# Inverse root by Ln and Exp on ScalarE, and the shift of the fp32 residual moved out of the tile chain

## The reference

```python
def layer_norm(x, g, b):
    mu = jnp.mean(xf, axis=-1, keepdims=True)
    var = jnp.mean(jnp.square(xf - mu), axis=-1, keepdims=True)
    y = (xf - mu) * lax.rsqrt(var + LN_EPS) * g + b
...
    x = layer_norm(DEEPNORM_ALPHA * x + mix, ln_g[i, 0], ln_b[i, 0])
    if i % 2 == 0:
        ff = swiglu(x, ffn_w_gu[i // 2], ffn_w_down[i // 2])
    else:
        ff = moe_swiglu(x, moe_w_router[i // 2], moe_w_gu[i // 2], moe_w_down[i // 2])
    x = layer_norm(DEEPNORM_ALPHA * x + ff, ln_g[i, 1], ln_b[i, 1])
    x = x + (p[i] @ ple_w_proj[i]) * jax.nn.sigmoid(x @ ple_w_gate[i])
```

## Time and profile before

| | |
|---|---|
| median of 3 runs | 1476.85 us (1471.23 to 1479.42) |
| the profiled execution | 1471.44 us |
| its span, first to last instruction | 1469.7 us |
| TensorE busy | 1324.6 us (90%) |
| VectorE busy | 648.9 us (44%) |
| ScalarE busy | 565.9 us (39%) |
| GpSimd busy | 150.0 us (10%) |

### The profile page before, as it was taken

One profiled execution on the slowest core, in us unless ns is written; L12 is line 12 of the kernel. 1 busy time (PEld: TensorE's weight loads), 2 busy tenths in 40 slices (PEclk: granted clock), 3 DMA queues, 4 the chain that ended last, 5 costly groups with the idle time before them and its releaser, 6 DMA issues.

```text
span 1469.7 us, 17566 instructions
## 1 busy us (share of the span) xinstructions
PE 1324.6 (90%) x6495; PEld 1106.7 (75%) x6496; DVE 648.9 (44%) x906; ACT 565.9 (39%) x783; POOL 150.0 (10%) x106
## 2 busy tenths in 40 slices
PE   7999879799999999998899998797879899988648
PEld 6889778488888878867787896673768798877537
DVE  5333554633333322336433337445553443455565
ACT  3222542632322322236332224234454554466642
POOL 0000000000000000000000000000233532255400
PEclk9999999999999999999999999897789999999869
DMA  6332003133333333203356520020685776588841
GB/s 186 103 101 87 15 15 87 34 97 105 94 99 101 102 99 98 73 29 115 86 92 81 83 76 1 29 65 9 210 263 188 258 230 197 181 275 283 315 158 58
DMA packets 197914, 175.46 MB, mean 119 GB/s; under 512 B 7201, under 2 KB 178273, under 8 KB 197857
## 3 DMA queue, kind: packets, MB, share of 16 engines
q1 hardware_dynamic: 194016, 160.53, 38.0%
q0 software_dynamic: 3312, 12.06, 2.2%
q10 hardware_dynamic: 528, 2.10, 0.4%
HBM read 164.71 MB, written 9.96 MB: 119 GB/s over the span
## 4 chain that ended last, share of the span: by engine, by line
PE 77%; DVE 7%; issue 6%; ACT 4%; DMA 3%; POOL 2%; POOLq 0%; SPq 0%; ACTq 0%; DVEq 0%
PE bank L705 24%; PE bank L706 23%; PE bank L707 23%; POOL w_lo L663 2%; PE bank L798 1%; DMA raw<-ple_w_gate 1%; DMA raw<-moe_w_down 1%; DVE rstd L1682 1%; PE bank L1017 1%; PE bank L872 1%; DVE w_lo L1598 1%; DMA x_tok<-x 1%; PE bank L876 1%; DVE sp L1784 0%; PE bank L934 0%
## 5 line engine op out<-in xcount | busy, mean ns | idle before, releaser
L1598 DVE TENSOR_TENSOR w_lo<-raw,w_hi 128x1024 fp32r<-128x1024 f32 (+5 forms) x215 | 300.5, 1404 | 317.0 <-ACT w_hi L1213 165.4
L705 PE MATMUL bank<-x_hi,w_hi 128*128 128x512 f32 x672 | 265.2, 395 | 15.6 <-DVE x_lo L1598 11.4
L706 PE MATMUL bank<-x_lo,w_hi 128*128 128x512 f32 x672 | 263.9, 393 | 0.0
L707 PE MATMUL bank<-x_hi,w_lo 128*128 128x512 f32 x672 | 263.7, 392 | 0.0
L1213 ACT CAST w_hi<-raw 128x1024 fp32r<-128x1024 f32 (+2 forms) x141 | 149.8, 1063 | 165.9 <-PE bank L707 159.3
L705 PE MATMUL bank<-w_hi,x_hi 128*128 128x256 f32 (+2 forms) x608 | 189.9, 312 | 9.3 <-DVE x_lo L1626 3.1
L706 PE MATMUL bank<-w_lo,x_hi 128*128 128x256 f32 (+2 forms) x608 | 188.1, 309 | 0.0
L707 PE MATMUL bank<-w_hi,x_lo 128*128 128x256 f32 (+2 forms) x608 | 188.0, 309 | 0.0
L705 PEld LDWEIGHTS bank<-x_hi,w_hi 128*128 128x128 f32 x672 | 127.7, 190 | 46.8 <-DVE w_lo L1598 9.5
L1486 ACT CAST w_hi<-raw 128x1536 fp32r<-128x1536 f32 (+2 forms) x98 | 130.1, 1338 | 75.8 <-PE bank L707 38.6
L707 PEld LDWEIGHTS bank<-x_hi,w_lo 128*128 128x128 f32 x672 | 127.6, 190 | 27.1
(11 more groups left out here) (287 smaller groups left out, 1879.9 us busy)
## 6 DMA issues: line engine op xcount, KB each, us to landing
raw<-moe_w_gu SPq DMA_DIRECT2D x32, 768.0 KB, 4.5
raw<-ffn_w_gu SPq DMA_DIRECT2D x44, 512.0 KB, 3.8
raw<-moe_w_gu SPq DMA_DIRECT2D x32, 640.0 KB, 4.2
raw<-a_w_qkv SPq DMA_DIRECT2D x24, 512.0 KB, 3.7
raw<-moe_w_down SPq DMA_DIRECT2D x16, 768.0 KB
raw<-ffn_w_down SPq DMA_DIRECT2D x16, 704.0 KB, 4.4
raw<-ple_w_gate SPq DMA_DIRECT2D x16, 512.0 KB, 4.1
raw<-kvf_w SPq DMA_DIRECT2D x16, 512.0 KB, 7.3
```

The lines of the kernel that those rows point to most:

```text
L705: pe.matmul(o, s_hi, m_hi, start=start, stop=False, skip_group_check=True)
L706: pe.matmul(o, s_hi, m_lo, start=False, stop=False, skip_group_check=True)
L707: return pe.matmul(o, s_lo, m_hi, start=False, stop=stop, skip_group_check=True)
L1598: return dve.tensor_tensor(dst, a, b, ALU.subtract)
```

## The change

The inverse root is taken as exp(-ln(var + eps) / 2) on ScalarE: Ln in the place of Sqrt, then Exp with scale -0.5, which now raises `rstd_ready`. VectorE's reciprocal is gone. Ln and Exp are in one table set, which attention has loaded before norms 0 and 2, so `norm` preloads it at norm 1 alone.

At norms 0 and 1 VectorE's scaling also multiplies by the gain column. ScalarE adds the shift only once in the chain, rounded into `x_hi`. VectorE adds it again, in fp32, where it makes `x_lo`. `x_exact` itself is left without its shift: after norm 0 ScalarE adds it inside gu, two tiles after each of the first four chunk steps (`shift_exact`); after norm 1 VectorE adds it in gate0, where it adds the embedding.

```diff
             def affine_tile(n, k):
...
-                if n != 2:
-                    act.activation(x_hi[:, k, :], x_exact[:, k, :], ACT.Identity, bias=b, scale=g)
-                act.activation(x_exact[:, k, :], x_exact[:, k, :], ACT.Identity, bias=b, scale=g).then_inc(affine, 1)
+                if n == 2:
+                    act.activation(x_exact[:, k, :], x_exact[:, k, :], ACT.Identity, bias=b, scale=g).then_inc(affine, 1)
+                else:
+                    act.activation(x_hi[:, k, :], x_exact[:, k, :], ACT.Identity, bias=b).then_inc(shifted, 1)
+
+            def shift_exact(k):
+
+                act.activation(x_exact[:, k, :], x_exact[:, k, :], ACT.Identity,
+                               bias=ln_cols[:, 32 + k:33 + k]).then_inc(affine, 1)
 
             def norm(n):
-                act.preload_act_table_set("sqrt_and_others")
+                if n == 1:
+                    act.preload_act_table_set("natural_log_exp_and_others")
...
-                act.activation(rstd[:, :], bank[5][:, :], ACT.Sqrt, bias=eps[:, 0:1]).then_inc(std_ready, 1)
+                act.activation(rstd[:, :], bank[5][:, :], ACT.Ln, bias=eps[:, 0:1]).then_inc(std_ready, 1)
+                act.wait_ge(std_ready, n + 1)
+                act.activation(rstd[:, :], rstd[:, :], ACT.Exp, scale=-0.5).then_inc(rstd_ready, 1)
...
             def gu_step(q, i, j, last):
                 ahead("gu", q, j, last)
+                if isinstance(i, int) and i == 0:
+                    act.wait_ge(x_ready, KD)
+                    shift_exact(2 * j)
+                    shift_exact(2 * j + 1)
...
                     elif j % 2:
                         dve.wait_ge(chunk_done, 4 * q + j + 1)
+                        dve.wait_ge(affine, KD)
...
-                dve.wait_ge(std_ready, n + 1)
-                dve.reciprocal(rstd[:, :], rstd[:, :]).then_inc(rstd_ready, 1)
...
-                    dve.tensor_tensor(x_exact[:, k, :], x_exact[:, k, :], rstd[:, :], ALU.mult).then_inc(normed, 1)
+                    if n == 2:
+                        dve.tensor_tensor(x_exact[:, k, :], x_exact[:, k, :], rstd[:, :], ALU.mult).then_inc(normed, 1)
+                    else:
+                        dve.scalar_tensor_tensor(out=x_exact[:, k, :], in0=x_exact[:, k, :],
+                                                 scalar=ln_cols[:, n * KD + k:n * KD + k + 1], in1=rstd[:, :],
+                                                 op0=ALU.mult, op1=ALU.mult).then_inc(normed, 1)
...
-                        dve.wait_ge(affine, done + k + 1)
-                        minus(x_lo[:, k, :], x_exact[:, k, :], x_hi[:, k, :].bitcast(F32)).then_inc(x_ready, 1)
+                        dve.wait_ge(shifted, KD * n + k + 1)
+                        dve.scalar_tensor_tensor(out=x_lo[:, k, :], in0=x_exact[:, k, :],
+                                                 scalar=ln_cols[:, 32 + n * KD + k:33 + n * KD + k],
+                                                 in1=x_hi[:, k, :].bitcast(F32), op0=ALU.add, op1=ALU.subtract
+                                                 ).then_inc(x_ready, 1)
...
-                    dve.tensor_tensor(x_exact[:, k, :], x_exact[:, k, :], proj[:, k, :], ALU.add).then_inc(embedded, 1)
+                    dve.scalar_tensor_tensor(out=x_exact[:, k, :], in0=x_exact[:, k, :],
+                                             scalar=ln_cols[:, 32 + KD + k:33 + KD + k], in1=proj[:, k, :],
+                                             op0=ALU.add, op1=ALU.add).then_inc(embedded, 1)
```

More of the change, by code:

```diff
@@ L360, in build @@
         normed = sem("normed")
+        shifted = sem("shifted")
         affine = sem("affine")
@@ L1015, in _ @@
             for k in range(KD):
-                pe.wait_ge(affine, 3 * KD + k + 1)
+                pe.wait_ge(affine, 2 * KD + k + 1)
                 mm = pe.matmul(bank[5][0:NE, :], w_r[:, k, :], x_exact[:, k, :], start=k == 0, stop=k == KD - 1)
@@ L1680, in norm @@
                     ahead("proj0", q_proj, 0, False)
-                dve.wait_ge(std_ready, n + 1)
-                dve.reciprocal(rstd[:, :], rstd[:, :]).then_inc(rstd_ready, 1)
                 dve.wait_ge(rstd_ready, n + 1)
                 dve.wait_ge(squared, KD * (n + 1))
-                done = [0, KD, 3 * KD, 4 * KD][n]
                 def scale(k):
-                    dve.tensor_tensor(x_exact[:, k, :], x_exact[:, k, :], rstd[:, :], ALU.mult).then_inc(normed, 1)
+                    if n == 2:
[4 more added lines that the diff above has]
+                                                 op0=ALU.mult, op1=ALU.mult).then_inc(normed, 1)
                 def low_tile(k):
                     if n != 2:
-                        dve.wait_ge(affine, done + k + 1)
-                        minus(x_lo[:, k, :], x_exact[:, k, :], x_hi[:, k, :].bitcast(F32)).then_inc(x_ready, 1)
+                        dve.wait_ge(shifted, KD * n + k + 1)
[3 more added lines that the diff above has]
+                                                 ).then_inc(x_ready, 1)
                 for k in range(KD):
@@ L1746, in gate @@
                     for k in range(KD):
-                        dve.wait_ge(affine, 2 * KD + k + 1)
+                        dve.wait_ge(affine, KD + k + 1)
                         minus(x_lo[:, k, :], x_exact[:, k, :], x_hi[:, k, :].bitcast(F32)).then_inc(x_ready, 1)
```

## The result

The kernel with the change takes 1466.47 us (median of 6 runs, 1461.98 to 1468.13) against 1475.40 us for the kernel before (6 runs, 1471.23 to 1479.42). The ratio is 0.9934, with a 95% interval of 0.9908 to 0.9959: 0.7% faster, 8.9 us. A second set of runs of the same kernel on another occasion gave 1466.85 us and 0.9942 (0.9916 to 0.9967). Of the 29 runs of the kernel before that stand beside the second group of experiments, one took 2652.94 us, and no ratio uses it.

The account below looks back on a forecast made before the run. A long run of split matmuls on TensorE (70% of the span) with three holes at the norms bounds the kernel. Gains of 2.1, 2.1 and 2.7 make 6.9, with the clock 9.1 us: 1476.85 - 9.1 = 1467.7 us, range 1459 to 1475.

Parts of the forecast that it names:

- Inverse root: Start of Ln to first scaling takes 1.38 us; gain 2.9 us at norm 0, 2.7 at norm 2.
- Tile chain: At norm 0 the fourth tile reaches TensorE 6.9 us after the first scaling instead of 7.3: gain 0.4 us.
- Shift moved into gu: In gu, four shifts queued on ScalarE delay the cast of chunk 3: loss 1.2 us (0.9 to 1.5).
- Norm 1: Before gate0, a shorter ScalarE queue lets TensorE restart at 673.8 instead of 675.92: gain 2.1 us.
- Norm 2: Before the router, tiles still pass one scaling and one affine, so only the root counts: gain 2.7 us.
- The rest: Three removed table loads were hidden; the fused add in gate0 costs nothing, 0.1 us at its last tile.
- TensorE's clock: No clock fall at the shorter holes of norms 1 and 2: worth 4.4 us, half counted, 2.2 us.
- Rival B: Clock returns nothing, routing takes it back, or gu's stall is at its upper end: gain 4.5 to 7.4 us; chance 0.22.
- Rival E: The three removed table loads had delayed their norms: 3.8 us more gain, 1463.9 us; chance 0.05.
- F: No gain: Ln and Exp take as long as the Sqrt and reciprocal they replace, 1476.9 us; chance 0.03.
- D: Slower: new rounding moves a token and an expert needs one more 128-token tile, 1497 us; chance 0.05.
- C: What norm 2 gains is lost in the expert stage: gain 4.2 us, 1472.7 us; chance 0.10.

Follow-up runs that it names:

- late shifts: The changed kernel with the eight shifts of x_exact as four and four behind the casts of gu's chunks 3 and 4: 1466.74 us, ratio 0.9942.
- the filled norm 1: The changed kernel with eight matmuls whose result nobody reads in TensorE's hole before gate0: 1466.31 us, ratio 0.9955.
- all holes filled: The changed kernel with late shifts and useless matmuls in four holes (norm 0, norm 1, before q1, norm 2): 1459.02 us, ratio 0.9888.

## Why the prediction was right, and where it wasn't

The forecast was a gain of 9.1 us; the medians moved by 8.9 and the profiled spans by 9.3. Against 1476.85 it came to 1467.7; measured, 1466.5. By its own steps:

- *Inverse root.* 1.38 us from Ln to the first scaling at all three norms, to the hundredth. The two rows it was built from, an Exp in attention and the gap between two such activations, carried over exactly. The experiment with the root alone shows the gains of 2.9 and 2.7 us at norms 0 and 2.
- *Tile chain.* Fourth tile 6.9 us after the first scaling as computed; VectorE's two operations take 0.74 us and start 0.66 apart, taken as 0.75 and 0.67. Worth 0.4 us there, seen in the experiment without the root (the fourth tile comes 18.9 us after the first square sum, against 19.3), and 0.6 at chunk 2.
- *Shift moved into gu.* The stall was there, at the chunk named, behind the instructions named: 1.01 us idle, 1.1 with the slower first matmul behind it, and 1.1 to 1.4 us of the whole stretch when undone, against 1.2 (0.9 to 1.5) in the sum. Norm 0 net: 2.1 forecast, 2.1 measured.
- *Norm 1.* The hole is 2.45 us, forecast 2.4, and the restart 2.1 us sooner. The two experiments that take the change apart show that the chain's queue brings 1.7 of it and the root the rest, which is how the step argued: Exp lies in idle time there, and the gain has to come from the queue.
- *Norm 2.* 3.0 us against 2.7. The extra 0.3 us goes with the chain: the three kernels with the old chain have a gap of 0.20 us among the square sums of norm 2, the seven with the new one have none, and chain and shift alone is 13.4 us there against 13.7. Why a chain that the norm 2 tiles don't take does that was not followed.
- *The rest.* The table loads were hidden: shown with five more of them. The fused add in gate0: nothing seen.
- *TensorE's clock.* **This is the step that failed in its rule, though its number held, which was in part luck.** "The new holes are 2.4 and 3.0 us, so I expect no fall": at norm 1 the clock fell all the same, 0.4 us after the restart, and its 1.3 us did not come. All five profiles with this hole of 2.45 us have a fall at it. The full amount, 1.6 us, came only when the hole was filled. At norm 2 it held in the changed kernel (twice) and with the root alone, and didn't with late shifts, in the filled norm 1 and with more table loads: 7.03, 7.03, 7.03 us against 9.96, 8.32 and 8.32, all after the same hole of 3.01 us. The rule rested on the first matmuls after two holes of 2.90 and 3.19 us, and a first matmul at full speed doesn't show that the clock holds. In the very trace that they come from, the clock was down 0.7 us after the one restart and 1.5 us after the other. This is the kernel before, behind the hole of 3.19 us that ends at 523.73:

```profile
525.60 0.63 PE L706 MATMUL bank<-h_lo,w_hi 128*128 128x512 f32 x1
```

  All ten profiles have these two holes, with no edit in them, and in all ten the mean granted clock over the 3 us from the restart is 0.50 to 0.75. Only where the fall comes differs. Behind the hole of 3.19 us it came 0.4 us after the restart in the first profile of the changed kernel, and before the restart in the second:

```profile
522.33 0.51 PE L706 MATMUL bank<-h_hi,w_hi 128*128 128x512 f32 x1 [3.19 <-DVE h_lo L1612]
```

```profile
521.71 0.79 PE L706 MATMUL bank<-h_hi,w_hi 128*128 128x512 f32 x1 [3.19 <-DVE h_lo L1612]
```

  The 2.2 us in the sum came out because only half was counted, on the ground that other executions have less to lose; it wasn't made up as forecast. The profile shows 3.0 us at the router and 1.2 in the rest of the routing stage, where small matmuls happened to be fast (1.95 us against 3.60), nothing at norm 1, and 1.1 us lost in two stretches that the change doesn't touch. The medians, over many executions, leave 8.9 - 6.9 = 2.0 us for it, with an interval of 3.8 us each way.

  The granted clock of every timed run is on record too. Among the runs of the kernel before, the longer ones have the lower clock (correlation -0.86 over 30 runs, -0.85 over 28), so most of what sets two executions of equal code apart goes with the clock. Its mean is 0.951 and 0.952 in these two sets, 0.952 with chain and shift alone, 0.955 with the root alone, 0.953 with late shifts and with norm 1 filled, 0.956 in both sets of the changed kernel and with more table loads, and 0.960 with all holes filled. So every kernel with the new root ran at a higher mean clock than the kernel before. One minus the clock, times the span, is the full-speed time lost: 72 us before, 65 us after. The difference of 7 us is the most that the clock can have brought, an estimate from these means, since part of the lost time falls into holes where it costs nothing. It doesn't say how much of the 7 us the change earned and how much was drawn: late shifts and the filled norm 1 run the same code elsewhere and lost 69 to 70 us.

Rival B, with no clock gain, isn't excluded by the medians, since 6.9 us lies inside the interval; the clocks of the runs speak against it. Rival E is excluded, since the loads cost nothing, and so is F: Ln takes 0.69 us and Exp 0.63. D didn't occur: the first expert product still runs 176 matmuls of each half-width form. C, a loss in the expert stage, isn't seen in the changed kernel (360.4 and 360.6 us against 359.8). That stage does range from 359.4 to 365.4 over all profiles, with no order in it by what was changed, a wider range than any other stretch without an edit has. The longest has the lowest granted clock over the stage (0.92) and two of the shortest, 359.4 and 360.0 us, have 0.94. What sets the clock there stays open.

What was not foreseen is that the parts are so unequal. The root alone gives all that can be measured (1464.7 us); the chain and the shift on top of it give 1.5 us at norm 1 and 0.3 at norm 2 and take 0.7 at norm 0 (380.8 against 380.0), about a microsecond net by the restarts and nothing by the medians. By the whole stretch norm 1 would be 2.8 us (79.8 against 77.0), but 1.3 of that is the root-alone profile's longer time at the low clock.

## What to carry to other kernels

An operation of an off-path engine that stands alone between two stages of the bound engine is worth all that it can be shortened by, and where the new instructions already have rows in the profile the gain can be predicted: here 2.9 and 2.7 us, right to the tenth. Where several queues feed one wait, ask which of them is late next before counting a gain: at norm 1 a quicker root gave 0.6 us and a shorter queue 1.7. And a hole in front of long matmuls costs more than its idle time: filling it with matmuls nobody needs was worth almost as much here (7.8 us, late shifts included) as the whole change. But it took all four holes: the one at norm 2 filled alone moved nothing. And the first matmul after a hole doesn't tell whether the clock holds; the next 1.5 us have to be read too.

## What the runs showed of the hardware

- The granted clock fell at very different times after TensorE's stop, in equal code. Behind two holes of 2.90 and 3.19 us it was down within 1.5 us of the restart, or already before it, in all ten profiles. After the stop at norm 2 it fell before the restart at 3.0 us in three kernels (means of 0.85 and 0.87 over the hole) and not before the router was done in two; at norm 1, after a hole of 2.45 us, it fell in all five profiles that have this hole, but at the restart in two, to within 0.2 us (the first matmul takes 0.78 and 0.80 us), and 0.4, 1 and 1.5 us after it in the others; at norm 0, after 4.30 us, it fell some 0.8 us after the restart in one profile and within 0.1 us of it in the next. The length of a hole alone doesn't decide it between 2.45 and 4.3 us. No hole that was filled down to 0.6 to 1.1 us was followed by a fall at its restart.
- Two table loads in a row take 1.28 us each with 0.01 between them, and in gu Silu starts at 291.50, 0.01 us after a load that ends at 291.49.
- A scalar_tensor_tensor with a column operand over 128x512 in fp32 takes 0.74 to 0.75 us and starts every 0.66, where a plain tensor_tensor takes 0.69 and starts every 0.60. An activation with one column operand takes 0.71 to 0.72 us, with two 0.80; four of the former took 2.56 us, 0.62 apart.
- The pace of a long run of equal matmuls can differ by 2% between kernels in a stage that both share (216 against 220 in 50 us, at a granted clock of 1.00 in both), seen once, without a cause found.
